# A fourth k-tile pair with seven block products in the up stage of a macaron FFN kernel

## What is computed

```python
D_MODEL = 2048; SEQ = 256; D_FF = 5632; FFN_RES_WEIGHT = 0.5

def swiglu(x, wg, wu, wd):
    return (jax.nn.silu(x @ wg) * (x @ wu)) @ wd

f = swiglu(rmsnorm(h, ffn1_pre_g[l]), ffn1_wg[l], ffn1_wu[l], ffn1_wd[l])
h = h + FFN_RES_WEIGHT * rmsnorm(f, ffn1_post_g[l])
...
f = swiglu(rmsnorm(h, ffn2_pre_g[l]), ffn2_wg[l], ffn2_wu[l], ffn2_wd[l])
h = h + FFN_RES_WEIGHT * rmsnorm(f, ffn2_post_g[l])
```

## Time and profile before

| | us |
|---|---|
| median of 3 runs | 2082.45 (2082.16 to 2082.65) |
| the profiled execution | 2081.73 |
| its span, first to last instruction | 2079.9 |
| PE busy in the span | 2067.6 |
| DVE busy in the span | 1680.6 |
| ACT busy in the span | 1111.2 |
| mean granted TensorE clock | 0.999 of full |

### The profile page before, as it was taken

The page is one execution under the profiler, slowest core; times in us unless marked ns, Lnnn a source line. Parts: engine busy times, 40 slices in busy tenths (PEclk is TensorE's granted clock), DMA queues, the critical chain, the costliest instruction groups (busy, mean ns, idle before and its releaser), DMA issues.

```text
span 2079.9 us, 25938 instructions
## 1 busy us (share of the span) xinstructions
PE 2067.6 (99%) x9322; PEld 1711.2 (82%) x9322; DVE 1680.6 (81%) x2049; ACT 1111.2 (53%) x1252; POOL 27.7 (1%) x54
## 2 busy tenths in 40 slices
PE   9999999999999999999999999999999999999998
PEld 8888888888888788888788888888888888888886
DVE  6889889889887658998687555578898888889885
ACT  6555555556555454444556444465555555565453
POOL 0000000000000000100000000000000000000000
PEclk9999999999999999999999999999999999999999
DMA  8666556666666566776655666556566665656564
GB/s 287 220 200 205 192 191 202 202 201 193 203 195 215 171 185 191 207 202 179 177 175 175 187 191 209 192 174 208 187 202 201 202 202 187 209 190 208 197 202 162
DMA packets 211996, 409.51 MB, mean 197 GB/s; under 512 B 15114, under 2 KB 15378, under 8 KB 211521
## 3 DMA queue, kind: packets, MB, share of 16 engines
q1 hardware_dynamic: 209904, 401.26, 60.4%
q0 software_dynamic: 1856, 7.01, 1.4%
q10 hardware_dynamic: 144, 0.04, 0.0%
HBM read 406.14 MB, written 2.11 MB: 196 GB/s over the span
## 4 chain that ended last, share of the span: by engine, by line
PE 95%; DVE 2%; DMA 1%; issue 1%; ACT 0%; SPq 0%; POOL 0%; DVEq 0%; ACTq 0%; POOLq 0%
PE banks L1544 93%; PE banks L1594 2%; DVE wlo L957 1%; DMA raw<-in_ffn_wu_dram 1%; DVE res L1012 0%; DMA raw<-in_ffn_wg_dram 0%; DVE act_lo L1025 0%; DVE wsum L1150 0%; DVE wsum L1155 0%; ACT act_hi L532 0%; ACT whi L517 0%; DVE nat L1138 0%; POOL stat L430 0%; DVE comb L1169 0%; DVE comb L1165 0%
## 5 line engine op out<-in xcount | busy, mean ns | idle before, releaser
L517 ACT ACTIVATE whi<-raw 128x1024 fp32r<-128x1024 f32 x755 | 779.7, 1053 | 734.6 <-PE banks L1544 372.1
L957 DVE TENSOR_TENSOR wlo<-raw,whi 128x1024 fp32r<-128x1024 f32 x756 | 900.2, 1218 | 258.9 <-ACT whi L517 255.8
L1544 PE MATMUL banks<-whi,act_hi 128*128 128x512 f32 x1688 | 541.7, 395 | 0.8 <-DVE wlo L957 0.7
L1544 PE MATMUL banks<-whi,act_lo 128*128 128x512 f32 x1688 | 532.0, 389 | 0.0
L1544 PE MATMUL banks<-wlo,act_hi 128*128 128x512 f32 x1688 | 522.3, 389 | 0.1
L1544 PEld LDWEIGHTS banks<-whi,act_lo 128*128 128x128 f32 x1688 | 316.9, 188 | 66.8
L1544 PEld LDWEIGHTS banks<-wlo,act_hi 128*128 128x128 f32 x1688 | 316.7, 188 | 66.7 <-DVE wlo L957 1.0
L1544 PEld LDWEIGHTS banks<-whi,act_hi 128*128 128x128 f32 x1688 | 313.6, 188 | 67.2 <-issue 4.7
L1544 PE MATMUL banks<-whi,h_hi 128*128 128x512 f32 x560 | 179.2, 390 | 0.0
L1544 PE MATMUL banks<-whi,h_lo 128*128 128x512 f32 x560 | 179.0, 389 | 0.0
L1544 PE MATMUL banks<-wlo,h_hi 128*128 128x512 f32 x560 | 174.9, 389 | 0.0
(11 more groups left out here) (239 smaller groups left out, 2017.7 us busy)
## 6 DMA issues: line engine op xcount, KB each, us to landing
raw<-in_ffn_wg_dram SPq DMA_DIRECT2D x176, 512.0 KB, 3.7
raw<-in_ffn_wu_dram SPq DMA_DIRECT2D x176, 512.0 KB, 4.6
raw<-in_ffn_wd_dram SPq DMA_DIRECT2D x176, 512.0 KB, 4.7
raw<-in_w_in_dram SPq DMA_DIRECT2D x160, 512.0 KB, 3.6
raw<-in_w_out_dram SPq DMA_DIRECT2D x32, 512.0 KB, 3.6
raw<-in_w_pw_dram SPq DMA_DIRECT2D x16, 512.0 KB, 3.7
raw<-in_w_o_dram SPq DMA_DIRECT2D x16, 512.0 KB, 3.7
x_t<-in_x_tiles_dram SPq DMA_DIRECT2D x8, 256.0 KB, 6.7
```

Of the source, the lines that this page charges most:

```text
L517: nc.scalar.activation(whi[:, j % RING, 0:kts * width], raw[:, j % RING, 0:kts * width], ACT.Copy).then_inc(hi_ready, 1)
L957: nc.vector.tensor_tensor(wlo[:, j % RING, 0:n], raw[:, j % RING, 0:n], whi[:, j % RING, 0:n], ALU.subtract).then_inc(lo_ready, 1)
L1544: return nc.tensor.matmul(o, a, b, **kw)
```

## The change

`SEVEN` becomes (1, 3, 5, 6), so in each of the ten summed chunks of both FFNs pair 6 is a seven-product pair directly behind pair 5, and `len(SEVEN)` is 4 wherever it counts. Around it:

- `combine` is done after pair 7, not after pair 6, and its last two adds are one instruction of 1024 elements with a broadcast and a reversed operand. ACT's two copies for it are after pair 7 too.
- `hidden` moves from behind pair 1 to behind the `lo`s of pair 6, ahead of that pair's `wsum_lo`; `gate_silu` from behind pair 1 to behind pair 4.
- `hidden_transpose` moves from behind pair 6 to behind pair 7. ACT's `hidden_copy` moves from the end of the chunk to behind pair 0's `hi`s of the next one, and PE's wait for it from the chunk's start to ahead of slab 1.
- `act_sums` makes four sets of sums instead of three in chunk 0 and shares one buffer for it (`afull`).

```diff
-SEVEN = (1, 3, 5)
+SEVEN = (1, 3, 5, 6)
...
+                def weight_sums_hi(seven, opens):
+
+                    act.wait_ge(wsum_ready, 4 * seven + 4)
+                    if not opens:
+                        act.wait_ge(wsum_used, seven)
+                    nc.scalar.activation(wsum_hi[:], wsum[:], ACT.Copy).then_inc(wsumhi_ready, 1)
...
+                        hi_at(2 * q + 1)
+                        if q in SEVEN:
+                            weight_sums_hi(seven, first and f == 0 and q == SEVEN[0])
+                        if q == 0 and not first:
+                            hidden_copy(c - 2, group)
+                        if q == 4 and not first:
                             gate_silu(c - 1)
-                        if q == 6:
-                            act.wait_ge(wsum_used, seven_before(f, c, len(SEVEN)))
-                            if first:
-                                act.wait_ge(acc_free[1], freed0[f][1] + 1)
-                            else:
-                                act.wait_ge(hidden_ready, SUMMED * f + c - 1)
-                            nc.scalar.activation(comb[:, C11, :], banks[:, 4 * (1 - group) + M1, :], ACT.Copy)
-                            nc.scalar.activation(comb[:, C22, :], banks[:, 4 * (1 - group) + M5, :],
-                                                 ACT.Copy).then_inc(outer_copied, 1)
-                    hidden_copy(c - 1, 1 - group)
+                    act.wait_ge(wsum_used, seven_before(f, c, len(SEVEN)))
+                    if first:
+                        act.wait_ge(acc_free[1], freed0[f][1] + 1)
+                    else:
+                        act.wait_ge(hidden_ready, SUMMED * f + c - 1)
+                    nc.scalar.activation(comb[:, C11, :], banks[:, 4 * (1 - group) + M1, :], ACT.Copy)
+                    nc.scalar.activation(comb[:, C22, :], banks[:, 4 * (1 - group) + M5, :], ACT.Copy).then_inc(outer_copied, 1)
...
                     quad(0, 2 * q, q)
+                    if q == 0:
+                        hidden_copy(SUMMED - 1, 1)
...
-                    link(nc.vector.tensor_tensor(afull[:, i], act_hi[:, h], act_lo[:, h], ALU.add))
+                    if i:
+                        dve.wait_ge(asum_ready, ASUMS * f + i)
+                    link(nc.vector.tensor_tensor(afull[:], act_hi[:, h], act_lo[:, h], ALU.add))
...
-                    nc.vector.tensor_tensor(comb[:, C12, :], comb[:, C22, :], comb[:, C12, :], ALU.subtract).then_inc(combined, 1)
-                    dve.wait_ge(combined, combined_count(f, c, 3))
-                    nc.vector.tensor_tensor(comb[:, C22, :], comb[:, C22, :], comb[:, C21, :], ALU.subtract).then_inc(combined, 1)
+                    nc.vector.tensor_tensor(comb[:, C12:C22 + 1, :], comb[:, C22:C22 + 1, :].to_broadcast([P, 2, CW]),
+                                            comb[:, C12:C11:-1, :], ALU.subtract).then_inc(combined, 2)
...
                         for j in 2 * q, 2 * q + 1:
                             lo(j, n0 + j + 1)
+                        if q == 6 and not first:
+                            hidden(c - 1)
                         if q in SEVEN:
                             weight_sums_lo(seven)
-                        if q == SEVEN[0] and not first:
-                            hidden(c - 1)
-                        if q == 6:
-                            combine(c, group)
+                    combine(c, group)
...
-                    if not first:
-                        pe.wait_ge(hf_ready, UP_CHUNKS * f + c - 1)
...
                             for j in 2 * q, 2 * q + 1:
+                                if j == 1 and not first:
+                                    pe.wait_ge(hf_ready, UP_CHUNKS * f + c - 1)
                                 slab(j, n0 + j + 1, 2 * group + j % 2, act_hi, act_lo, SK * q, KT - 1)
-                        if q == 6:
+                        if q == UP_SLABS // 2 - 1:
                             pe.wait_ge(combined, combined_count(f, c, 2))
                             hidden_transpose(c - 1, 1 - group, first)
```

More of the change, by code:

```diff
@@ L169, in build @@
         asum_hi, _ = sb("asum_hi", [P, len(SEVEN), 4, P], f32r)
-        asum_lo, _ = sb("asum_lo", [P, len(SEVEN), 4, P], f32r)
-        asum, _ = sb("asum", [P, len(SEVEN), 4, P])
-        afull, _ = sb("afull", [P, len(SEVEN), TT, 2, P])
+        asum_lo, o_asum_lo = sb("asum_lo", [P, len(SEVEN), 4, P], f32r)
+        asum, _ = sb("asum", [P, len(SEVEN), 4, P], over=o_asum_lo)
+        afull, _ = sb("afull", [P, TT, 2, P])
         wsum_lo, _ = sb("wsum_lo", [P, 3, CW], f32r)
@@ L642, in hidden_copy, with hi_at @@
                     nc.scalar.activation(h_f[:, bass.ds(KB * c, KB), :], spare_blocks(group), ACT.Copy).then_inc(hf_ready, 1)
+                def weight_sums_hi(seven, opens):
[3 more added lines that the diff above has]
+                    nc.scalar.activation(wsum_hi[:], wsum[:], ACT.Copy).then_inc(wsumhi_ready, 1)
                 def summed(c, group):
                     first = isinstance(c, int) and c == 1
+                    def hi_at(j):
+                        hi(j, base + UP_SLABS * c + j - RING + 1, base // RING + UP_SLABS // RING * c + j // RING + 1)
@@ L646, in summed @@
                     for q in range(UP_SLABS // 2):
                         seven = seven_before(f, c, SEVEN.index(q)) if q in SEVEN else None
[L648 to L651, removed]
+                        hi_at(2 * q)
                         if q in SEVEN:
[L653 to L656, removed]
@@ L657, in summed @@
-                        if q == 1 and not first:
-                            gate_silu(c - 1)
-                        if q == 6:
-                            act.wait_ge(wsum_used, seven_before(f, c, len(SEVEN)))
-                            if first:
-                                act.wait_ge(acc_free[1], freed0[f][1] + 1)
-                            else:
-                                act.wait_ge(hidden_ready, SUMMED * f + c - 1)
-                            nc.scalar.activation(comb[:, C11, :], banks[:, 4 * (1 - group) + M1, :], ACT.Copy)
-                            nc.scalar.activation(comb[:, C22, :], banks[:, 4 * (1 - group) + M5, :],
-                                                 ACT.Copy).then_inc(outer_copied, 1)
@@ L668, in summed @@
-                    hidden_copy(c - 1, 1 - group)
+                            act.wait_ge(wsum_ready, 4 * seven + 3)
+                        hi_at(2 * q + 1)
[4 more added lines that the diff above has]
+                        if q == 4 and not first:
+                            gate_silu(c - 1)
+                    act.wait_ge(wsum_used, seven_before(f, c, len(SEVEN)))
@@ L1112, in act_sums @@
                     h = SEVEN[i]
-                    link(nc.vector.tensor_tensor(afull[:, i], act_hi[:, h], act_lo[:, h], ALU.add))
-                    a11, a12, a21, a22 = (afull[:, i, t, k, :] for t in range(TT) for k in range(2))
+                    if i:
+                        dve.wait_ge(asum_ready, ASUMS * f + i)
+                    link(nc.vector.tensor_tensor(afull[:], act_hi[:, h], act_lo[:, h], ALU.add))
+                    a11, a12, a21, a22 = (afull[:, t, k, :] for t in range(TT) for k in range(2))
                     link(nc.vector.tensor_tensor(asum[:, i, S5, :], a21, a22, ALU.subtract))
@@ L1735, in quad @@
                         for o in range(2):
+                            if half == 0 and q == 0 and o:
+                                pe.wait_ge(hf_ready, UP_CHUNKS * f + SUMMED)
                             down_slab(n + o, q, 2 * (1 - half) + o)
-                pe.wait_ge(hf_ready, UP_CHUNKS * f + SUMMED)
                 for q in range(DOWN_SLABS):
```

## The result

The changed kernel takes 2093.37 us (median of 7, 2088.40 to 2095.68) against 2082.39 us before: a ratio of 1.0049, 95% interval 1.0038 to 1.0060. It is 11 us slower, where 2082.0 was forecast and the range ended at 2092. The profiled execution has a span of 2092.7 us against 2079.9, 12.8 us more.

The account below looks back on a forecast made before the run. PE bounds the kernel before; afterwards DVE's 42.4 us chunk exceeds PE's 41.6. Per FFN PE saves 6.8 us and waits 6.6, net −0.4 us in both: 2082.0 us beside the median of 2082.45, range 2072 to 2092.

Parts of the forecast that it names:

- PE's saving: Pair 6 of each summed chunk: three matmuls fewer, 0.68 us a pair, 13.6 us over twenty chunks.
- PE's wait for `wsum_lo`: Ahead of pair 6's last three matmuls: one new PE wait per chunk, 0.8 to 1.0 us.
- The load waits: DVE ahead of `weight_sums` in pairs 5 and 3: waits of 0.73 and 0.56 us for up-weight loads.
- the forecast case: DVE's load waits in pairs 3 and 5 sum to 1.1 to 1.6 us: 2078.3 to 2086.6 us, chance 0.43.
- rival (d): DVE's load waits in pairs 3 and 5 are 0.99 us each as in chunk 1: 2094 us, chance 0.28.
- What DVE waits for: DVE's idle time per chunk: two waits vanish, load waits remain, making its chunk 42.4 us from 41.06 us of work.
- The lead of 0.8 us, once per FFN: DVE can be at most 0.8 us early for pair 6's `wsum_lo`, taken off PE's waits once per FFN.
- PE's chunk: PE's work per up-stage chunk after the change: 42.30 − 0.68 = 41.62 us.
- The sum itself: Per FFN: PE saves 6.8 us and waits 9 × 0.82 − 0.8 = 6.6 us, net −0.2 us.
- Edits that cost nothing: Moved copies, `hidden_copy`, silu and chunk 0's fourth set of activation sums were all taken as covered, costing nothing.
- the cover that I had called thin: Ahead of `combine`, ACT's copies hidden behind pair 7's `lo`s by 0.17 us; each 0.1 us beyond costs 1.8 us.
- the prediction's 3.4 us: Estimated landing time of the second of two 512 KB loads issued 1.0 us apart; neither pair 3 nor 5 would wait.

Follow-up runs that it names:

- the last kernel: Changed kernel with `hidden` split behind pairs 1 and 3, ACT's first copy early, second `wsum` buffer, last chunk's silu one pair later in the down stage: 2070.44 us, ratio 0.9944.
- The second buffer: Changed kernel with a second `wsum` buffer for pair 6, all else as it was: 2088.26 us, ratio 1.0025.
- moving silu: Last chunk's `gate_silu` one pair later in the down stage, against the kernel with the moves alone: 2081.69 us, ratio 0.9997.
- the kernel with the moves alone: Changed kernel with `SEVEN` = (1, 3, 5) again, every move kept: 2084.31 us, ratio 1.0009.
- all three experiments that moved `hidden`: Changed kernel with `hidden` back behind pair 1 (2086.89 us), ahead of pair 6's sums (2092.43 us), or in halves behind pairs 1 and 3 (2080.93 us).
- the quarter-load kernel: Changed kernel whose summed-chunk loads bring 128 of 512 columns, compute instructions unchanged: 2071.92 us, ratio 0.9950.

## Why the prediction was wrong

**What held.** PE's saving: 0.68 us a pair, 13.6 us in all; the last kernel is 11.9 us faster than the one beside it. The bound passes from PE to DVE, through its waits for loads in pairs 3 and 5, and DVE's work per chunk (41.1 us busy). PE's wait for `wsum_lo` is where it was put. The load waits were forecast at 0.73 us in pair 5 and 0.56 in pair 3, 1.3 together; over the eighteen chunks they are 0.76 and 0.70 by starts, 1.46 together. That lies in the band of the forecast case (1.1 to 1.6), not in that of rival (d). Rival (d), slower, at 2094, has the time, but its main reason, load waits of 0.99 us as in chunk 1, did not come. Its second reason, "any other small wait of DVE that the tight order makes", had no price and is what happened. That its time is so near is luck.

**What failed.** The step was "What DVE waits for": it counted idle time that the trace of before showed, and took the new order as free of others, so DVE's chunk was put at 42.4 us and is 42.96, 10 us too little over the eighteen chunks 2 to 10. Forecast against measured, the first four for these 10 us:

- *The wait of pair 6's first add for pair 5's `wsum_lo`*: put at nothing, measured 0.28 us × 16 + 0.11 × 2 = 4.7 us. The second buffer gave 5.1 us back, chunk 1 included. In the trace of before no `weight_sums` follows a `wsum_lo` directly, so no row had it; the change's own order of rows did show the two in a row.
- *`combine`*: put at 2.58 us; the distance from its second to its third instruction, put at 0.72 us, is 0.79, and 0.91 or more in four of FFN 1's chunks. Some 2 us together; no run took this apart.
- *The loads*: 1.46 us a chunk in pairs 3 and 5, where 1.34 was the forecast with the 0.05 of pair 1, which hardly came. About 2 us together.
- *Not assigned*: some 1 us of the 10.
- *The lead of 0.8 us, once per FFN*: it was not there, 1.6 us. In FFN 1's chunk 1 PE even loses about 1.4 us; in FFN 2's it loses nothing, and the lead is not there either.
- *PE's chunk*: 41.69 us, not 41.62. I had taken a 42.30 us window for the period, which is 42.37. Some 1.3 us the other way.
- *The sum itself*: it used 0.82 us of wait a chunk, where its terms give 42.40 − 41.62 = 0.78. Together with 0.5 us that the kernel before loses in its own chunks 2 to 10, 1.2 us the other way.

**"Edits that cost nothing" was wrong in two places.** I looked at silu and the moved `combine` only inside the loop. At the down stage's start they cost 1.3 us in each FFN; moving silu gave back 2.6 us in the kernel with the moves alone. The fourth set of activation sums, said to fall where PE never waits, costs PE a few tenths in FFN 1's chunk 1. And the cover that I had called thin, 0.17 us ahead of `combine`, held in the changed kernel only because `hidden` delays DVE there. It broke in all three experiments that moved `hidden`, and they fell short by about that.

Together: 10 for DVE's chunk (4.7 `wsum`, about 2 `combine`, about 2 loads, 1 not assigned), 3.0 for the lead and chunk 1, 2.7 at the down starts, less 1.3 and 1.2, is 13 us over the forecast's −0.4. The profiled execution is 12.8 us longer than before, 13.2 over the forecast.

The Trainium skill, "DMA: Bandwidth & Descriptors", section "Anatomy of one DMA", gives the fit behind the prediction's 3.4 us for transfers that GpSimd issues. The loads here are issued on SP's queue, and the second of a pair took 3.7 to 4.9 us to land in the kernel before and 3.8 to 5.3 in the changed one.

## What to carry to other kernels

When a change moves the bound to another engine, write that engine's new list down and ask at each neighbouring pair whether the second needs the first's buffer or result; the old trace has no row for neighbours that the change makes. An engine whose work fills its period is slowed by every wait for a load, and by every path that leads from it over other engines back to it; short independent instructions belong ahead of exactly those waits. And follow a moved step out of the loop into the code behind it.

## What the runs showed of the hardware

A load of 512 KB issued as the second of a pair lands after 3.8 to 5.3 us in the changed kernel (71 loads of FFN 1's chunks), mostly near 3.9 or near 4.7; one of 128 KB lands after 2.2 us in the quarter-load kernel. The kernel before, with PE as the bound, varied by 1 us over 7 runs, though its loads scatter too (3.7 to 4.9). The changed kernel, with DVE as the bound and waiting for these loads, varies by 7 us over 7 runs, and with quarter loads by 0.5 us over 4.

Of two 128 x 512 adds on DVE the second starts 0.72 us after the first if it waits on a semaphore for it, and 0.61 us if it need not (the first three adds of a `weight_sums` in the changed kernel: 234.70, 235.42, 236.03). A `weight_sums` behind the `wsum_lo` it must wait for starts 0.28 us later than one that need not, in a hardware loop, and 0.11 us later in the chunks written out; what makes the difference no run shows.
